# One block fewer in an input projection, and eight transposes fewer in a delta rule

## The reference

```
# gated delta rule, in chunks of 128 columns in the kernel
S = S * gt + einsum(kt, v_new)          # the state after a chunk: keys of that chunk as rows of tokens
# odd layer
u = x @ od_w_in                          # 1024 -> 1968 columns
gq, gk, gv, g_low, gr, c_q, c_kv, k_r = split(u)   # 256,256,512,16,512,256,128,32
yc = gla_mixer(gq, gk, gv, g_low, gr, ...)          # its gate: g_low (16 columns) @ w_gate
yd = mla_mixer(c_q, c_kv, k_r, ..., cos, sin)       # k_r: 32 rotary columns of the key
# rotary: k_r * cos + (k_r with its halves exchanged) * (-sin, sin)
```

## Time and profile before

| | |
|---|---|
| median of 3 runs | 1445.23 us (1445.07 to 1447.6) |
| profiled execution, span from first to last instruction | 1443.1 us (its own total isn't shown) |
| PE busy | 1423.5 us, 99% |
| DVE busy | 1013.4 us, 70% |
| ACT busy | 779.4 us, 54% |
| POOL busy | 294.0 us, 20% |
| mean granted TensorE clock | 0.999 of full speed |
| read from memory | 221.32 MB, 154 GB/s over the span |

### The profile page before, as it was taken

How to read it: one execution, slowest core, us unless ns; L and a number is a source line. 1 busy time by engine, 2 the same in 40 slices (tenths; PEclk the granted TensorE clock), 3 DMA queues, 4 the chain that set the end, 5 groups by cost and what they waited for, 6 DMA issues and landing times.

```text
span 1443.1 us, 31771 instructions
## 1 busy us (share of the span) xinstructions
PE 1423.5 (99%) x11333; PEld 1363.9 (95%) x11333; DVE 1013.4 (70%) x1701; ACT 779.4 (54%) x1399; POOL 294.0 (20%) x348
## 2 busy tenths in 40 slices
PE   9999999999999999999999999999999999999997
PEld 8999888899999999999999999999999989999986
DVE  7884957659876477569888477587664687776645
ACT  6556324556655366466565356464453567654542
POOL 3804002103444000002544000013330012033310
PEclk9999999999999999999999999999999999999999
DMA  7551231244655535344666544546556433565552
GB/s 256 177 175 47 88 101 47 93 142 160 190 175 175 175 119 189 103 146 128 193 189 189 182 134 152 164 146 200 183 168 204 152 116 118 163 217 186 183 180 91
DMA packets 60996, 223.57 MB, mean 155 GB/s; under 512 B 6768, under 2 KB 6896, under 8 KB 60528
## 3 DMA queue, kind: packets, MB, share of 16 engines
q1 hardware_dynamic: 60624, 220.17, 48.1%
q10 hardware_dynamic: 288, 2.23, 0.4%
HBM read 221.32 MB, written 1.05 MB: 154 GB/s over the span
## 4 chain that ended last, share of the span: by engine, by line
PE 81%; DVE 12%; issue 3%; ACT 3%; DVEq 1%; ACTq 0%; POOL 0%; POOLq 0%
PE bank L440 20%; PE bank L441 20%; PE bank L442 20%; DVE wlo L415 3%; PE bank L461 2%; PE bank L1168 2%; PE bank L462 1%; PE bank L468 1%; DVE bank L947 1%; PE bank L3284 1%; PE bank L3285 1%; PE bank L3287 1%; ACT cv L831 1%; DVE cv L839 1%; DVE work L1782 1%
## 5 line engine op out<-in xcount | busy, mean ns | idle before, releaser
L415 DVE TENSOR_TENSOR wlo<-raw,whi 128x1024 fp32r<-128x1024 f32 x397 | 501.4, 1268 | 249.3 <-ACT whi L410 248.8
L410 ACT ACTIVATE whi<-raw 128x1024 fp32r<-128x1024 f32 x397 | 415.1, 1056 | 288.6 <-PE bank L442 240.6
L440 PE MATMUL bank<-xs,whi 128*128 128x258 f32 (+2 forms) x1984 | 569.2, 287 | 0.0
L441 PE MATMUL bank<-xs,whi 128*128 128x258 f32 (+2 forms) x1984 | 563.9, 284 | 0.0
L442 PE MATMUL bank<-xs,wlo 128*128 128x258 f32 (+2 forms) x1984 | 561.6, 283 | 0.0
L440 PEld LDWEIGHTS bank<-xs,whi 128*128 128x128 f32 x1984 | 374.2, 189 | 3.0 <-issue 1.6
L442 PEld LDWEIGHTS bank<-xs,wlo 128*128 128x128 f32 x1984 | 375.0, 189 | 0.0
L441 PEld LDWEIGHTS bank<-xs,whi 128*128 128x128 f32 x1984 | 374.3, 189 | 0.6 <-issue 0.2
L440 PE MATMUL bank<-hf,whi 128*128 (+3 forms) x848 | 241.3, 285 | 2.0 <-DVE cv L839 0.8
L441 PE MATMUL bank<-hf,whi 128*128 (+3 forms) x848 | 240.3, 283 | 0.0
L442 PE MATMUL bank<-hf,wlo 128*128 (+3 forms) x848 | 240.2, 283 | 0.0
(11 more groups left out here) (516 smaller groups left out, 1671.8 us busy)
## 6 DMA issues: line engine op xcount, KB each, us to landing
raw<-stream SPq DMA_DIRECT2D x412, 512.0 KB, 3.7
con<-consts SPq DMA_DIRECT2D x1, 1284.5 KB, 10.5
big<-mla ACTq DMA_DIRECT2D x1, 1152.0 KB, 7.8
hs_sb<-hs SPq DMA_DIRECT2D x2, 544.0 KB, 4.2
work<-last ACTq DMA_DIRECT2D x1, 1024.0 KB, 9.1
y_out<-work SPq DMA_DIRECT2D x4, 256.0 KB, 2.0
par<-params SPq DMA_DIRECT2D x1, 420.0 KB, 7.9
par<-params SPq DMA_DIRECT2D x1, 224.0 KB, 4.8
```

The source lines that it names most:

```text
L410: nc.scalar.activation(whi[:, s, :], raw[:, s, :], ACT.Copy).then_inc(hi_split, 1)
L415: nc.vector.tensor_tensor(wlo[:, s, :], raw[:, s, :], whi[:, s, :].bitcast(F32), ALU.subtract).then_inc(block_split, 1)
L440: nc.tensor.matmul(out_, whi[:, slot, w], hi, start=start, stop=False)
L441: nc.tensor.matmul(out_, whi[:, slot, w], lo, start=False, stop=False)
```

## The change

Tile 15 has free rows. The rotary key columns with exchanged halves move there, to rows 96 to 127, and tile 16 and its block go: 16 blocks in place of 17, and 411 in the stream. `mla_rope_key` reads the second product's operand from rows 96 to 127 of tile 15, with a copy of the sine table in the same rows. The lists of PE, ACT and DVE are numbered anew: what stood behind the gate stays in order, and ahead of the gate stand tiles 0 to 4 where tiles 0 to 5 stood. PSUM banks and slots shift by one. In the delta rule the keys of the second chunk aren't transposed, and ACT copies 128 columns where it copied 256.

```diff
-OD_TILES = tuple(range(12, 17)) + (2, 3, 0, 1, 4, 5, 6, 7, 8, 9, 10, 11)
+OD_TILES = tuple(range(12, 16)) + (2, 3, 0, 1, 4, 5, 6, 7, 8, 9, 10, 11)
...
-    cos, sin = np.ones((96, T2), np.float32), np.zeros((96, T2), np.float32)
+    cos, sin = np.ones((96, T2), np.float32), np.zeros((P, T2), np.float32)
...
+    sin[96:128] = sin[64:96]
...
-    odw = np.concatenate([od[:, :1024], od[:, 1040:1936], od[:, 1024:1040], none, kr, none[:, :32]] + [kr[:, SWAP]] * 4, 1)
+    odw = np.concatenate([od[:, :1024], od[:, 1040:1936], od[:, 1024:1040], none, kr, kr[:, SWAP]], 1)
...
-    ktok = lambda k, c: flat(cv[:, :, :])[:, k * 256 + (c - 1) * P:k * 256 + c * P]
+    ktok = lambda k: flat(cv[:, :, :])[:, k * P:(k + 1) * P]
...
-            for c in (1, 2):
-                last = tr(bank[5][:, (c - 1) * P:c * P], at(kn, c), ident)
-            last.then_inc(*m.mark(f"kt{k}"))
+            tr(bank[5][:, 0:P], at(kn, 1), ident).then_inc(*m.mark(f"kt{k}"))
...
-            A(flat(cv[:, :, :])[:, 256 * k:256 * k + 256], bank[5][:, 0:256], ACT.Copy).then_inc(*a_.mark(f"kt{k}"))
+            A(ktok(k), bank[5][:, 0:P], ACT.Copy).then_inc(*a_.mark(f"kt{k}"))
...
-    OD_FIRST = 5
-    OD_SCALE = (0.125, 0.125) + (1.0,) * 15
+    OD_FIRST = 4
+    OD_SCALE = (0.125, 0.125) + (1.0,) * 14
...
     def odd_pe(pe):
         tile = lambda t: od_tile_pe(pe, t)
-        tile(5)
+        tile(4)
         gla_gate_pe(pe)
         mla_norm_pe(pe)
+        tile(5)
         tile(6)
-        tile(7)
         gla_cumulate_pe(pe)
...
     def odd_act(act):
...
         tile(3)
         tile(4)
-        tile(5)
         act.wait_ge(*m.at("gate"))
...
         mla_norm_act(act)
+        tile(5)
+        residual_act(act, 1, "ln_ffn", 0)
         tile(6)
-        residual_act(act, 1, "ln_ffn", 0)
-        tile(7)
...
-        od_copied(dve, 4)
-        tt(tmp96[64:96], big[64:96, 16, 0:T2], sin[64:96], ALU.mult).then_inc(*v.mark("kr1"))
+        tt(tmp96[64:96], big[96:128, 15, 0:T2], cn("sin")[96:128], ALU.mult).then_inc(*v.mark("kr1"))
```

More of the change, by code:

```diff
@@ L136 @@
           ("ev_in", "tiles", 18), ("ev_out", "wide", 8), ("up2", "tiles", 44), ("down2", "wide", 22),
-          ("od_in", "tiles", 17), ("od_out", "wide", 8), ("up3", "tiles", 44), ("down3", "wide", 22)]
+          ("od_in", "tiles", 16), ("od_out", "wide", 8), ("up3", "tiles", 44), ("down3", "wide", 22)]
 FIRST_BLOCK, _n = {}, 0
@@ L1008, in build @@
                     ("ev_in", 6), ("ev_out", 8), ("lm0", 1), ("lv0", 1), ("up2", 44), ("down2", 8), ("lm1", 1), ("lv1", 1),
-                    ("od_in", 5), ("od_out", 8), ("lm2", 1), ("lv2", 1), ("up3", 44), ("down3", 8), ("lm3", 1), ("lv3", 1)):
+                    ("od_in", 4), ("od_out", 8), ("lm2", 1), ("lv2", 1), ("up3", 44), ("down3", 8), ("lm3", 1), ("lv3", 1)):
         G[name] = _g
@@ L1473, in outputs @@
                     pe.wait_ge(*v.at(f"S{n - 1 if n != 8 else 3}"))
-                mm(bank[6][:, 0:256], ktok(k, 1), vd_buf[n % 2][:, :], start=True, stop=True).then_inc(*m.mark(f"s{n}"))
+                mm(bank[6][:, 0:256], ktok(k), vd_buf[n % 2][:, :], start=True, stop=True).then_inc(*m.mark(f"s{n}"))
         def squares(g, heads):
@@ L2423, in ev_in_act @@
             nc.scalar.activation(big[:, 12 + t, 0:T2], bank[(g0 + t) % 8][:, 0:T2], ACT.Copy).then_inc(bank_free, 1)
-    OD_FIRST = 5
-    OD_SCALE = (0.125, 0.125) + (1.0,) * 15
+    OD_FIRST = 4
+    OD_SCALE = (0.125, 0.125) + (1.0,) * 14
     _o = lambda n: bank[(G["od_in"] + n) % 8]
-    OD_C, OD_X = [_o(n) for n in (7, 0, 1, 2, 3, 4)], [_o(5), _o(6)]
+    OD_C, OD_X = [_o(n) for n in (6, 7, 0, 1, 2, 3)], [_o(4), _o(5)]
     od_bank = lambda t: _o(t) if t < OD_FIRST else OD_X[(t - OD_FIRST) % 2]
@@ L2862, in odd_pe @@
         tile = lambda t: od_tile_pe(pe, t)
-        tile(5)
+        tile(4)
         gla_gate_pe(pe)
         mla_norm_pe(pe)
+        tile(5)
         tile(6)
-        tile(7)
         gla_cumulate_pe(pe)
         mla_heads_pe(pe)
+        tile(7)
+        mla_values_pe(pe)
         tile(8)
-        mla_values_pe(pe)
-        tile(9)
         mla_scores_pe(pe, 0)
         mla_scores_pe(pe, 1)
+        tile(9)
         tile(10)
+        mla_transposes_pe(pe, 0)
         tile(11)
-        mla_transposes_pe(pe, 0)
-        tile(12)
         mla_transposes_pe(pe, 1)
         mla_outputs_pe(pe, 0)
-        tile(13)
+        tile(12)
         mla_outputs_pe(pe, 1)
         gla_values_pe(pe)
+        tile(13)
+        gla_scores_pe(pe, PARTS)
         tile(14)
-        gla_scores_pe(pe, PARTS)
         tile(15)
-        tile(16)
         gla_outputs_pe(pe)
@@ L2891, in od_banks_read @@
         if bank[b] in OD_X:
-            pe.wait_ge(*S("od", "act").at(f"tile{15 + OD_X.index(bank[b])}"))
+            pe.wait_ge(*S("od", "act").at(f"tile{14 + OD_X.index(bank[b])}"))
         elif bank[b] in OD_C[0:2]:
@@ L2955, in odd_act @@
         gla_keys_act(act, (0,))
-        tile(8)
+        tile(7)
         act.wait_ge(*dp.at("v"))
@@ L2960, in odd_act @@
         gla_keys_act(act, (1, 2))
+        tile(8)
+        exps(0)
         tile(9)
-        exps(0)
-        tile(10)
         exps(1)
         transposed(0)
-        tile(11)
+        tile(10)
         transposed(1)
@@ L2969, in odd_act @@
         gla_keys_act(act, (4, 5, 3))
-        tile(12)
+        tile(11)
         def values():
@@ L2976, in values @@
                 A(vg[:, j, :], OD_C[2 + j][:, :], ACT.Copy).then_inc(*a_.mark(f"vt{j}"))
-        od_tile_act(act, 13, values)
-        tile(14)
+        od_tile_act(act, 12, values)
+        tile(13)
         act.wait_ge(*d.at("out1"))
@@ L2983, in odd_act @@
         nc.scalar.preload_act_table_set(SILU)
-        tile(15)
-        for t in range(13, 16):
+        tile(14)
+        for t in range(12, 15):
             od_copied(act, t)
@@ L2988, in odd_act @@
         A(r, r, ACT.Silu).then_inc(*a_.mark("ra"))
-        tile(16)
-        od_copied(act, 16)
+        tile(15)
+        od_copied(act, 15)
         A(big[:, 11, 0:T2], big[:, 11, 0:T2], ACT.Silu).then_inc(*a_.mark("r"))
@@ L3028, in odd_dve @@
         dve.wait_ge(*S("norm", "act").at("ln1v_scale"))
-        for t in range(6):
+        for t in range(5):
             tile(t)
@@ L3039, in odd_dve @@
         mla_norm_dve(dve)
+        tile(5)
+        residual_dve(dve, 1, "ln_ffn", 0)
         tile(6)
-        residual_dve(dve, 1, "ln_ffn", 0)
-        tile(7)
         dve.wait_ge(*a_.at("b"))
@@ L3050, in odd_dve @@
         keys(0, 1)
-        tile(8)
+        tile(7)
         keys(2)
-        od_product(dve, 9)
+        od_product(dve, 8)
         mla_masked(dve, 0)
         mla_masked(dve, 1)
-        od_product(dve, 10)
+        od_product(dve, 9)
         mla_weights(dve, 0)
         mla_weights(dve, 1)
-        od_product(dve, 11)
-        od_low(dve, 9)
+        od_product(dve, 10)
+        od_low(dve, 8)
         keys(4, 5)
         keys(3)
-        od_product(dve, 12)
-        for t in (10, 11, 12):
+        od_product(dve, 11)
+        for t in (9, 10, 11):
             od_low(dve, t)
@@ L3067, in odd_dve @@
         tt(QG, QG, big[:, 0:2, 0:T2], ALU.mult).then_inc(*v.mark("qg"))
+        tile(12)
         tile(13)
+        masks()
         tile(14)
-        masks()
         tile(15)
-        tile(16)
         for k in range(4):
@@ L3131, in mla_heads_pe @@
         pe.wait_ge(mla_loaded, 16)
-        od_copied(pe, 4)
+        od_copied(pe, 3)
         for h in range(4):
```

## The result

The changed kernel takes 1449.58 us (median of 6 runs, 1448.26 to 1453.14), the kernel before on the same chip 1445.03 (6 runs, 1444.79 to 1447.6): a ratio of 1.0028, 95% interval 1.0018 to 1.0038. The prediction was 1446.4 within 1443.4 to 1447.8, so it is wrong: the change costs about 0.3%, where I had given 7 in 100 to any cost above 0.2%.

A forecast was written before the change was run, and what follows sets the result against it. PE, busy for 99% of the span, was taken as the bound. 1445.2 - 2.87 (block) + 2.87 (pause) - 0.46 (delta loop) + 1.7 (clock) = 1446.4 us, range 1443.4 to 1447.8.

The forecast's parts named there:

- The block: Odd projection ahead of the gate: 2.87 us of removed PE work and a new 3.45 us pause cancel, 0 us.
- That the clock falls: At the pause ahead of the gate: the clock falls to half rate, chance 0.48, total 1446.4 us.
- the rival in which the clock holds: Pause ahead of the gate comes but the clock stays up: 1444.8 us, chance 0.32.
- the price of the clock: Behind the pause, from the gate on: 3.65 us at half rate lose 1.8; taken as +1.7 us, bounds 0 and 2.2.
- the start's 4.4 us: Kernel's start: 20 matmuls of 128x256 took 6.60 us, read as 2.2 us lost, 4.4 us at half rate.
- The 0.75: Part of the 4.4 us at half rate expected to lie inside the pause ahead of the gate and cost nothing.
- The rival that I gave 0.07: Gate, norm and two tiles behind: low clock lasts longer, above 6.7 us, or another new wait; slower, chance 0.07.
- The delta loop: Delta rule's set-up loop: -0.55 for transposes, -0.06 for copies, 0.15 given back; -0.46 us, bounds -1.0 and 0.
- the last three transposes: Delta set-up, L1279: of eight removed, these lie under ACT's part of the chain and are worth nothing.
- 0.03 us for a halved copy: Delta set-up, L1579: a copy of 128x128 in place of 128x256 saves 0.01 to 0.06 us, taken as 0.03.
- the copies' 0.06: Delta set-up: two of the eight halved copies lie on the chain, 0.06 us saved for both.
- The rotary key's 0: `mla_rope_key` reading tile 15 in place of tile 16: same products and sums, done before the queries need them, 0 us.

The follow-up runs named there:

- experiment 1: Changed kernel with both transposes of every key and the wide copy kept, so only the block is removed: 1449.67 us, ratio 1.0023 to the kernel before.
- first profile: Profile of the unedited changed kernel from its first measurement (median 1449.58 us); the profiled execution took 1451.3 us.
- experiment 10: Changed kernel with the missing block taken from between the score matmuls and the second mixer's first transposes, not ahead of the gate: 1444.16 us, ratio 0.9986.
- experiment 12: Changed kernel with the block taken out as in experiment 10 and the set-up's query squares moved as in experiment 5: 1443.0 us, ratio 0.9978.
- experiment 7: Changed kernel with three pairs of query-square matmuls in the delta set-up moved ahead of the wait for the token transposes: 1449.36 us, ratio 1.0018.
- experiment 8: Kernel of experiment 7 with 13 unread 128x256 matmuls behind the pause, ahead of the gate's first matmul: 1450.88 us, ratio 1.0029.
- second profile: Profile of the unedited changed kernel run again on another chip (experiment 4); the profiled execution took 1448.86 us, its set-up at the full clock.
- Experiment 9: Kernel of experiment 7 with 40 unread 128x256 matmuls behind the pause, ahead of the gate's first matmul: 1450.46 us, ratio 1.0036.
- experiment 2: Kernel before with one key transpose in place of two and the halved copy, 17 blocks kept: 1445.17 us, ratio 0.9992.
- experiment 4: Changed kernel again, unedited, on another chip than experiments 1 to 3: 1449.89 us, ratio 1.0027.
- experiment 5: Kernel before with three pairs of query-square matmuls in the delta set-up moved ahead of the wait for the token transposes: 1444.44 us, ratio 0.9989.
- experiment 3: Changed kernel with 27 unread 128x256 matmuls filling the pause ahead of the gate: 1445.11 us, ratio 0.9993.
- experiment 6: Changed kernel with 14 unread 128x256 matmuls in the pause ahead of the gate, in place of 27: 1447.25 us, ratio 1.0007.

## Why the prediction was wrong, by its steps

**The block: right.** Removed work and new pause cancel, as experiment 1 shows with the block alone. The wait on the gate is 3.3 us (3.4 forecast), ACT's stretch 6.13 us; the odd stage starts 1.99 us later than before in the first profile and the gate 1.98. Experiments 10 and 12 show the other side of this step: where another cover is taken, part of the block's 2.87 us does come through.

**That the clock falls: right, and more certain than I put it.** I gave it 0.48 against 0.32. In all eight profiles with the pause of 3.3 us it fell; it held with 2.1, 1.7 and 1.6 us, and fell with 2.8. All fourteen runs of the changed kernel lie at 1448.26 or above, over 3 us from the 1444.8 of the rival in which the clock holds, so that rival is out for it. With the same pause in edited kernels one run at 1446.28 (experiment 7) and one at 1446.18 (experiment 8), both with a mean clock of 0.998, lost less or nothing; neither has a profile.

**The step that failed: the price of the clock, +1.7 us with a bound of 2.2.** From the gate to the tile it measured 2.93 us in the first profile and 3.10 in the second, where it is 3.22 with the tile's first matmuls. The half rate was right and the duration mis-sized: I took the start's 4.4 us, less 0.75 in the pause, and the low stretch was 6.83 us, at least 6.24 of it outside the pause (in both profiles of the changed kernel). The 0.75 rested on a fall 2.7 us after the last matmul, read once, at the kernel's end; by the records of the clock in the eight profiles the fall came 2.1 to 4.1 us after the last matmul ahead of the pause, in five of them not before PE's next one. And the start was the wrong row to transfer the length from. There PE runs 20 wide matmuls end to end; behind this pause it runs 16 row and 128 column matmuls. Experiment 9 is nearest to the start, and its low stretch was 3.41 us. That the small matmuls alone are the cause is not shown: with 13 wide ones ahead of them the one profile has 13.65 us, and I can't say what sets 3.41, 6.83 or 13.65 us. The rival that I gave 0.07 put the border at 6.7 us low; it was the case that came, by 0.13 us. The Trainium skill ("TensorE: Matmul & The Clock Gate", "Terms") states the penalty as the throttled time times the share of the clock that is lost, so half of it at half rate; by that estimate the 6.24 low us behind the start of the gate make 3.1, and the trace's 2.93 is close to it.

**The delta loop: its sum right, by luck in part.** 17.25 to 16.79 us is the -0.46 of the forecast, and experiment 2's lower group agrees, but two of its terms were wrong. I let the last three transposes lie under ACT's part of the chain of waits. In the first profile of the changed kernel the chain stays with PE past the place in the sixth head where ACT had taken over before (137.85 in the earlier trace rows), and two more transposes lie on it:

```profile
139.96 0.11 PE bank L1279
...
141.66 0.11 PE bank L1279
...
143.13 0.47 ACT mix L1570
```

And I took 0.03 us for a halved copy. ACT's next instruction starts 0.16 us behind it, where it was 0.27 (138.99 to 139.26 in the earlier trace rows), so a copy saves 0.11:

```profile
141.01 0.29 ACT L1578 ACTIVATE cv<-bank 128x128 f32<-128x128 f32 x1
141.17 0.41 ACT L1597 ACTIVATE big<-bank 128x256 f32<-128x256 f32 x1
```

From the second head's first product to the end of the sixth head's exponents 12.33 us became 11.99; the other 0.12 came behind that place, where I had only the copies' 0.06.

**Not in my sum: two small terms.** 0.7 us at L2768 in the second profile and 0.4 us behind the last matmul. With them and the clock the sum would be 1445.2 - 0.5 + 3.2 + 0.7 + 0.4 = 1449.0; the profiled execution of experiment 4 took 1448.86. The clock's 3.2 alone would have made 1447.9, only just outside the range. The rotary key's 0 was not measured by itself.

**Not in my range: the spread.** In about half of its executions the kernel before, by experiments 2 and 5, and in some the kernel after, has a fall of the clock in the delta set-up, which costs 2.48 us in the first profile. The profile of before that I worked from has none, so the earlier trace rows couldn't show it. The spread of the three runs, 1445.07 to 1447.6, could have.

## What to carry to other kernels

Before taking work off the busiest engine, find out what it covers: here the block's time became a pause of the same length, and the pause put the next stage on half the clock. The price of a fall is half of the time at the low level where PE is full, as at the gate (6.83 us, 3.2 lost), and less where PE had waits to take up, as in the set-up (6.83 us, 2.48 lost; PE is busy for 2.95 of the 4.00 us from 122 to 126 in the kernel before). The time at the low level was 4.4 us at the start by my estimate and 3.41, 6.83 and 13.65 us elsewhere, so a length read at one place is no bound for another. When work must go, choose the place where the next wait is shortest and doesn't hang on a transfer; the same change cost 0.3% with the block taken at the gate and gained 0.14% with it taken between the scores and the transposes.

## What the runs showed of the hardware that was not expected

The clock falls without a long pause of PE, too: in the set-up rows PE is busy to 3.00 of 3.00 us at a clock of 0.51, and its only wait for another engine in the 3 us ahead of the fall is 0.56 us long. In those 3 us PE was busy for 2.44 us in experiment 2, with 19 matmuls; with the moved squares in experiment 5 it was busy for 3.00, with 25, and none of the eleven runs lay in the upper group. But the kernel before has 2.44 us in its own profile, in which the clock stayed up. So this stretch doesn't tell in which executions the clock falls. The two rows, of experiment 2 and of the kernel before:

```profile
116.00:119.00 3.00, 2.44 (x19) 1.94 (x18) 0.43 (x1) 2.12 (x6) 0.74 (x3) 1.00 0.60 180
...
116.00:119.00 3.00, 2.44 (x18) 1.88 (x17) 0.43 (x1) 1.74 (x6) 0.41 (x2) 1.00 0.62 180
```

The wait without a releaser on L2768 stands ahead of matmuls of 64x16, which start 0.02 us apart (24 in 0.57 us). In all seven profiles of kernels with PE's 11301 matmuls and the block taken out ahead of the cumulation, matmuls behind it are another 0.4 to 1.0 us late; in the eight kernels that have 8 to 40 matmuls more than the kernel after (experiments 1, 2, 3, 5, 6, 8, 9 and the kernel before) they aren't, nor in experiments 10 and 12, where the order differs. Instructions come in loads: the page of the profile has 59 on one queue, 0.97 MB, so 16 KB each. The Trainium skill ("Advanced Engine Details and Errata", "ISA Cache") gives lines of 16 KB, 256 instructions; the 16 KB agree.

```profile
q8 instruction: 59, 0.97, 0.3%
```

A load of this queue starts at 1210.63 us in the first profile and at 1208.26 in the second; the held matmuls start 2.4 us later in both, at 1213.07 and 1210.62. That fewer instructions ahead shift the loads against this dense place fits the rows; it was not tested by itself. The 0.4 us behind the last matmul came with every kernel that has the block removed, and with none that keeps it. It lies behind the last transfer, whose last packet ends 1.1 us ahead of the end of the span in those kernels and 0.7 in the three others; its cause is open as well.
